# Layer 1's retention: queries decayed by VectorE out of the score banks, keys zero-padded to 128 rows, the head loop one half piece sooner

## The reference, cut to what matters

```python
def _retention_dir(q, k, v, log_g, inclusive):      # chunks of 128 tokens
    ...
    dmat = jnp.where(mask[None], jnp.exp(log_g[:, None, None] * jnp.maximum(diff, 0).astype(jnp.float32)), 0.0)
    xi = jnp.exp(log_g[:, None] * (n + 1).astype(jnp.float32))
    zeta = jnp.exp(log_g[:, None] * (RET_CHUNK - 1 - n).astype(jnp.float32))
    ...
    def step(state, qkv):
        qc, kc, vc = qkv
        inner = jnp.einsum('bhqk,bhkv->bhqv', jnp.einsum('bhqd,bhkd->bhqk', qc, kc) * dmat, vc)
        cross = jnp.einsum('bhqd,bhdv->bhqv', qc * xi[..., None], state)
        new_state = chunk_decay[:, None, None] * state + jnp.einsum('bhkd,bhkv->bhdv', kc * zeta[..., None], vc)
        return new_state, inner + cross
```

## Time and profile before

| what | us |
|---|---|
| three executions | 814.00, 814.11, 814.99 |
| median | 814.11 |
| span of the profiled execution, first to last instruction | 811.6 |
| TensorE busy in it | 805.4 (99%) |
| VectorE busy | 634.0 (78%) |
| ScalarE busy | 339.9 (42%) |
| GpSimd busy | 187.8 (23%) |

### The profile page before, as it was taken

How to read it: one execution, slowest core, us unless ns; L and a number is a source line. 1 busy time by engine, 2 the same in 40 slices (tenths; PEclk the granted TensorE clock), 3 DMA queues, 4 the chain that set the end, 5 groups by cost and what they waited for, 6 DMA issues and landing times.

```text
span 811.6 us, 11794 instructions
## 1 busy us (share of the span) xinstructions
PE 805.4 (99%) x4364; PEld 691.4 (85%) x4364; DVE 634.0 (78%) x1112; ACT 339.9 (42%) x721; POOL 187.8 (23%) x189
## 2 busy tenths in 40 slices
PE   9999999999999999999999999999999999999998
PEld 7788888888888888888888888888889988999986
DVE  5998778768984476885578788978798678599998
ACT  4374465632122254342545544551134222455580
POOL 2222111111121221122324555544260114000000
PEclk9999999999999999999999999999999999999999
DMA  7236644445143322336868677596935634866562
GB/s 241 88 96 233 233 155 156 151 161 182 53 156 114 95 78 78 90 93 130 177 144 163 140 151 161 131 182 135 202 104 183 182 98 135 235 184 183 184 203 78
DMA packets 132862, 120.47 MB, mean 148 GB/s; under 512 B 4749, under 2 KB 100550, under 8 KB 132806
## 3 DMA queue, kind: packets, MB, share of 16 engines
q1 hardware_dynamic: 124326, 102.94, 40.9%
q0 software_dynamic: 8448, 16.78, 12.4%
q10 hardware_dynamic: 32, 0.01, 0.0%
HBM read 117.62 MB, written 35.65 MB: 189 GB/s over the span
## 4 chain that ended last, share of the span: by engine, by line
PE 92%; DVE 5%; issue 1%; ACT 1%; DMA 1%; POOL 0%; DVEq 0%; ACTq 0%
PE proj L1886 23%; PE proj L1888 23%; PE proj L1887 23%; PE bank_t L1900 3%; PE bank_o L1975 2%; DVE x L1592 1%; PE score L1888 1%; PE score L1887 1%; PE score L1886 1%; DVE w_lo L1247 1%; PE score L2050 1%; PE score L1960 1%; PE score L1961 1%; PE score L2049 1%; PE bank_o L2068 1%
## 5 line engine op out<-in xcount | busy, mean ns | idle before, releaser
L1247 DVE TENSOR_TENSOR w_lo<-w_raw,w_hi 128x1024 fp32r<-128x1024 f32 x151 | 192.0, 1274 | 44.3 <-POOL w_hi L778 36.1
L778 POOL TENSOR_SCALAR w_hi<-w_raw 128x1024 fp32r<-128x1024 f32 x101 | 118.6, 1174 | 438.6 <-DMA w_raw<-in_w_in_dram 314.6
L1886 PE MATMUL proj<-xt_hi,w_hi 128*128 128x512 f32 (+1 forms) x448 | 171.2, 382 | 0.0
L1888 PE MATMUL proj<-xt_hi,w_lo 128*128 128x512 f32 (+1 forms) x448 | 168.1, 375 | 0.0
L1887 PE MATMUL proj<-xt_lo,w_hi 128*128 128x512 f32 (+1 forms) x448 | 167.8, 374 | 0.0
L1888 PEld LDWEIGHTS proj<-xt_hi,w_lo 128*128 128x128 f32 x448 | 84.4, 188 | 15.6
L1887 PEld LDWEIGHTS proj<-xt_lo,w_hi 128*128 128x128 f32 x448 | 84.5, 189 | 14.1
L1886 PEld LDWEIGHTS proj<-xt_hi,w_hi 128*128 128x128 f32 x448 | 84.5, 189 | 14.0
L1886 PE MATMUL proj<-w_hi,xt_hi 128*128 128x512 f32 x152 | 60.9, 401 | 0.2 <-ACT prob L1012 0.2
L1888 PE MATMUL proj<-w_hi,xt_lo 128*128 128x512 f32 x152 | 59.5, 391 | 0.0
L1887 PE MATMUL proj<-w_lo,xt_hi 128*128 128x512 f32 x152 | 59.4, 391 | 0.0
(11 more groups left out here) (471 smaller groups left out, 1871.2 us busy)
## 6 DMA issues: line engine op xcount, KB each, us to landing
w_raw<-in_w_in_dram SPq DMA_DIRECT2D x79, 512.0 KB, 3.8
w_sums<-in_w_in_dram SPq DMA_DIRECT2D x8, 1024.0 KB, 7.0
w_sums<-w_sums POOLq DMA_DIRECT2D x8, 1024.0 KB, 9.1
w_raw<-w_sums SPq DMA_DIRECT2D x16, 512.0 KB, 3.8
w_raw<-w_sums SPq DMA_DIRECT2D x32, 256.0 KB, 3.3
w_raw<-in_w_out_dram SPq DMA_DIRECT2D x14, 512.0 KB, 3.3
w_raw<-in_w_in_dram SPq DMA_DIRECT2D x26, 256.0 KB, 3.3
w_sums<-in_w_attn_out_dram SPq DMA_DIRECT2D x4, 1024.0 KB, 6.5
```

What stands on the lines that cost most here:

```text
L778: pool.tensor_scalar(hi, raw, 1.0, 1.0, ALU.mult, ALU.mult).then_inc(hi_done, 1)
L1247: dve.tensor_tensor(lo, raw, hi.bitcast(F32), ALU.subtract).then_inc(w_split, 1)
L1886: pe.matmul(out, left[0], right[0], start=first, stop=False)
L1888: return pe.matmul(out, left[1], right[0], start=False, stop=last)
```

## The change

Queries are turned undecayed (RT 2, 3 are what RT 6, 7 were), ACT copies them to rqT, and VectorE multiplies the same bank by `decays` (a new table, the decay of each of 128 tokens, same on all partitions) into q_decT: two directions by two heads, so four instructions of 64 x 512 for each RT, eight in all. RN 2, 3 and RT 4 to 7 are gone. The keys of each head get a tile of 128 rows, rk_own, with the other head's 64 rows set to zero: ACT copies each key bank twice, with a per-partition scale of ones and zeros (half_of), and RS contracts over 128 rows. `decays` is built by VectorE (one instruction of 128 x 128 for each direction and head beside dmat, and two to begin with) and exponentiated by ACT in one instruction of 128 x 1024. RT 0 to 3 now stand at g = 17 and 18 ahead of AV and AN; KV, RS, RA and RB of each head stand one to three halves sooner. In the new list g = 19 and 20 have no TensorE step, g = 21 is KV 0, RS 0, F 0 in this order, and g = 22 is F 1.

```diff
 DA_FIRST = 4 * U_RQK
-RET_FIRST = DA_STEPS + 6
-RET_NORMS = (RET_FIRST + 3, RET_FIRST + 5, RET_FIRST + 9, RET_FIRST + 11)
+RET_FIRST = DA_STEPS + 5
+RET_NORMS = (RET_FIRST + 3, RET_FIRST + 5, RET_FIRST + 7, RET_FIRST + 9)
 WIN_FIRST = 4 * U_Z0 + 5
...
     g = 2 * (n - DA_FIRST) + half
+    x = 2 * (g - DA_STEPS - 1)
+    if 0 <= x < 4:
+        out += [("RT", x), ("RT", x + 1)]
     if 3 <= g < DA_STEPS + 3:
...
         out.append(("RN", g - 10))
-    if g == DA_STEPS:
-        out += [("RN", 2), ("RN", 3)]
-    x = 2 * (g - DA_STEPS - 1)
-    if 0 <= x < 8:
-        out += [("RT", x), ("RT", x + 1)]
     h, odd = divmod(g - RET_FIRST, 2)
...
             out.append(("RA", h - 1))
-    finals = {21: 0, 22: 1, 23: 2, 25: 3, 27: 4, 29: 5, 34: 6, 36: 7}
+    finals = {21: 0, 22: 1, 23: 2, 25: 3, 27: 4, 29: 5, 32: 6, 34: 7}
     if g in finals:
...
         diff = sb("diff", [P, TAB], stack=one)
-        rkT = sb("rkT", [P, 2, S], stack=one)
         k_decay = sb("k_decay", [P, ST, RET_HEADS, 2, HD], stack=one)
         dmat = sb("dmat", [P, RET_HEADS, P], stack=one)
+        decays = sb("decays", [P, 2, RET_HEADS, P], stack=one)
         lam_s = sb("lam_s", [P, 2], stack=one); lam_e = sb("lam_e", [P, 2], stack=one); neg_lam = sb("neg_lam", [P, 1], stack=one)
...
         dec_z = sb("dec_z", [P, 8], stack=one); dec_q = sb("dec_q", [P, 8], stack=one); dec_p = sb("dec_p", [P, 8], stack=one)
-        log_g = sb("log_g", [P, 8], stack=one); steps_to = sb("steps_to", [P, 4], stack=one)
-        ret_c = sb("ret_c", [P, 6, RET_HEADS], stack=one); rs_k = sb("rs_k", [P, ST], stack=one)
+        log_g = sb("log_g", [P, 8], stack=one); steps_to = sb("steps_to", [P, 2], stack=one); half_of = sb("half_of", [P, 2], stack=one)
+        ret_c = sb("ret_c", [P, 4, RET_HEADS], stack=one); rs_k = sb("rs_k", [P, ST], stack=one)
         neg_log_b = sb("neg_log_b", [P, 4], stack=one)
...
         decay_arg = sem("decay_arg"); decay_done = sem("decay_done")
-        ret_scaled = sem("ret_scaled")
+        ret_scaled = sem("ret_scaled"); q_decayed = sem("q_decayed"); halves_set = sem("halves_set")
         rt_done = sem("rt_done"); rt_free = sem("rt_free")
...
                 act.wait_ge(rt_done, m + 1)
-                if m == 6:
+                if m == 0:
+                    act.wait_ge(halves_set, 4)
+                if m == 2:
                     act.wait_ge(av_done, DA_STEPS)
-                dst = rkT[:, m, :] if m < 2 else q_decT[:, m - 2, :] if m < 6 else rqT[:, m - 6, :]
-                act.activation(dst, score[:, m % 2, :], ACT.Copy).then_inc(rt_free, 1)
+                if m < 2:
+
+                    for c in range(2):
+                        last = act.activation(rk_own[:, 2 * m + c, :], score[:, m % 2, :], ACT.Copy, scale=half_of[:, c:c + 1])
+                else:
+                    last = act.activation(rqT[:, m - 2, :], score[:, m % 2, :], ACT.Copy)
+                last.then_inc(rt_free, 1)
...
                         act.activation(dmat[:], dmat[:], ACT.Exp).then_inc(decay_done, 1)
+                        act.activation(decays[:], decays[:], ACT.Exp).then_inc(decay_done, 1)
...
                 minus_p = diff[:, CENTRE:CENTRE + 1]
-                for k, (sign, steps) in enumerate(((-1.0, 1.0), (1.0, P), (1.0, P - 1.0), (-1.0, 0.0))):
+                for c in range(2):
+                    here, there = halves(c)
+                    dve.memset(half_of[here, c:c + 1], 1.0).then_inc(halves_set, 1)
+                    dve.memset(half_of[there, c:c + 1], 0.0).then_inc(halves_set, 1)
+                for k, (sign, steps) in enumerate(((1.0, P - 1.0), (-1.0, 0.0))):
                     dve.tensor_scalar(steps_to[:, k:k + 1], minus_p, sign, float(steps), ALU.mult, ALU.add).then_inc(dve_chain, 1)
                     chain[0] += 1
                 dve.wait_ge(dve_chain, chain[0])
-                for k in range(4):
-                    dve.tensor_scalar(ret_c[:, k, :], log_g[:, 4 * (k % 2):4 * (k % 2) + 4], steps_to[:, k:k + 1], None, ALU.mult)
-                dve.tensor_scalar(ret_c[:, 4:6, :], log_g[:].rearrange("p (c h) -> p c h", c=2), float(P), None, ALU.mult).then_inc(decay_arg, 1)
+                for k in range(2):
+                    dve.tensor_scalar(ret_c[:, k, :], log_g[:, 4 * k:4 * k + 4], steps_to[:, k:k + 1], None, ALU.mult)
+                last_row = RET_HEADS - 1
+                done(dve.tensor_scalar(decays[:, 0, last_row, :], diff[:, CENTRE:CENTRE + P], minus_p, 1.0, ALU.subtract, ALU.add))
+                done(dve.tensor_scalar(decays[:, 1, last_row, :], decays[:, 0, last_row, :], -1.0, P + 1.0, ALU.mult, ALU.add))
+                dve.tensor_scalar(ret_c[:, 2:4, :], log_g[:].rearrange("p (c h) -> p c h", c=2), float(P), None, ALU.mult).then_inc(decay_arg, 1)
...
                 near = diff[:, CENTRE:CENTRE + P]
+                for c in range(2):
+                    dve.tensor_scalar(decays[:, c, h, :], decays[:, c, RET_HEADS - 1, :], log_g[:, 4 * c + h:4 * c + h + 1], None, ALU.mult)
                 done(dve.tensor_scalar(dmat[:, h, :], near, neg_log_b[:, h:h + 1], None, ALU.mult))
...
                                 wait_evacuated(dve, U_RQK, j)
-                        c = m % 2
-                        src = rqk[:, :, 256:512] if m < 2 else rqk[:, :, 0:256]
-                        dve.tensor_tensor((k_decay if m < 2 else q_decay)[:, :, :, c, :], src.rearrange("p s (h d) -> p s h d", h=RET_HEADS),
-                                          ret_c[:, 2 + c if m < 2 else c, :].unsqueeze(1).unsqueeze(3).broadcast_to([P, ST, RET_HEADS, HD]),
+                        dve.tensor_tensor(k_decay[:, :, :, m, :], rqk[:, :, 256:512].rearrange("p s (h d) -> p s h d", h=RET_HEADS),
+                                          ret_c[:, m, :].unsqueeze(1).unsqueeze(3).broadcast_to([P, ST, RET_HEADS, HD]),
                                           ALU.mult).then_inc(ret_scaled, 1)
+                    elif kind == "RT" and m >= 2:
+
+                        if m == 2:
+                            dve.wait_ge(decay_done, 3)
+                        dve.wait_ge(rt_free, m + 1)
+                        for c in range(2):
+                            here, h = slice(c * HD, (c + 1) * HD), 2 * (m - 2) + c
+                            for d in range(2):
+                                last = dve.tensor_tensor(q_decT[d * HD:(d + 1) * HD, h, :].rearrange("p (s q) -> p s q", s=ST),
+                                                         score[here, m % 2, :].rearrange("p (s q) -> p s q", s=ST),
+                                                         decays[here, d, h, :].unsqueeze(1).broadcast_to([HD, ST, P]), ALU.mult)
+                        last.then_inc(q_decayed, 1)
                     elif kind == "KV":
...
                         for k in (1, 2):
-                            dve.scalar_tensor_tensor(out=state[k + 1][f, :], in0=state[k][f, :], scalar=ret_c[f, 4, m:m + 1],
+                            dve.scalar_tensor_tensor(out=state[k + 1][f, :], in0=state[k][f, :], scalar=ret_c[f, 2, m:m + 1],
                                                      in1=kv[k][f, :], op0=ALU.mult, op1=ALU.add)
-                            back = dve.scalar_tensor_tensor(out=state[2 - k][b, :], in0=state[3 - k][b, :], scalar=ret_c[b, 5, m:m + 1],
+                            back = dve.scalar_tensor_tensor(out=state[2 - k][b, :], in0=state[3 - k][b, :], scalar=ret_c[b, 3, m:m + 1],
                                                             in1=kv[3 - k][b, :], op0=ALU.mult, op1=ALU.add)
...
                             wait_evacuated(pe, U_RQK, j)
-                    if m == 2:
-                        pe.wait_ge(ret_scaled, 4)
                     for s in range(ST):
                         if m < 2:
                             src = rqk[:, s, 256 + m * P:256 + (m + 1) * P]
-                        elif m < 6:
-                            src = q_decay[:, s, m - 2, :, :].rearrange("p c d -> p (c d)")
                         else:
-                            src = rqk[:, s, (m - 6) * P:(m - 5) * P]
+                            src = rqk[:, s, (m - 2) * P:(m - 1) * P]
                         last = pe.transpose(score[:, m % 2, s * P:(s + 1) * P], src, ident[:])
...
                     if m == 0:
-                        pe.wait_ge(rt_free, 8)
+                        pe.wait_ge(rt_free, 4)
+                        pe.wait_ge(q_decayed, 1)
+                        pe.wait_ge(ret_scaled, 2)
                         for j in range(ST):
...
                         pe.wait_ge(kr_free, 2 * m)
-                    r = slice((m % 2) * HD, (m % 2 + 1) * HD)
+                    else:
+                        pe.wait_ge(q_decayed, 2)
                     for c in range(ST):
-                        last = pe.matmul(score[:, 1, c * P:(c + 1) * P], rkT[r, m // 2, c * P:(c + 1) * P],
-                                         rqT[r, m // 2, c * P:(c + 1) * P], start=True, stop=True)
```

(4 more changed lines are left out.)

## The result

The changed kernel takes 830.69 us (median; 828.49 to 832.15), before 814.55 beside it: ratio 1.0189, interval 1.0164 to 1.0213, so 16.1 us slower. The profiled execution took 828.49 us, the shortest of the four; its span is 826.5, against 811.6 before.

A forecast was written before the change was run, and what follows sets the result against it. TensorE, busy 99% of the span, was taken to bound the kernel. Saving -3.5, waits +1.3 and +4.9, a pause +0.7, clock or third wait +1.5 gave +4.9: 814.1 to 819.0 us, range 816.2 to 822.4.

The forecast's parts named there:

- TensorE's saving: TensorE loses 3.5 us: 1.74 for RT 4 to 7, 1.4 for RS, 0.36 for fewer starts behind steps.
- the 1.4 for the padding: RS over 128 rows instead of 64 runs as AV does, saving 0.35 us per head, 1.4 for four.
- Rival 3: Padded keys give nothing, RS stays at 1.09 us, forecast otherwise holds: +0.8, 819.8 us; 12%.
- VectorE at g = 18: Eight multiplications ahead of AN, 0.61 us apiece, 4.9 in all, from 172.3 to 177.2.
- a pause: VectorE's small instructions sometimes take 0.7 us more; one taken in the gapless chain from 172.3 to 191.0.
- The waits at F 0 and F 1: TensorE waits 1.3 us at F 0 for ON 0 and 4.9 at F 1 for F 0 taken out.
- Rivals 1 and 2: 1: all VectorE work stays hidden, 810.6 us, 8%. 2: VectorE's multiplications cost half, 814.5 us, 8%.
- 5: Rival: the change doesn't do what it says, transposes stay or keys aren't padded; near 820 us, 1%.
- Rival 4: Both clock (2.4 us) and third wait (1.6 left at F 7), with two pauses: +8.1, 822.2 us; 10%.
- The third wait: TensorE at F 7 waits 0 to 2.6 us for F 6 taken out; 1.5 taken together with the clock.
- The clock: TensorE's clock may halve in the 4.9 us wait, costing 2.4 if lasting as long; 1.5 shared with third wait.

The follow-up runs named there:

- late multiplications: Changed kernel with retention at its old places, ACT copying queries to both halves, VectorE multiplying 128 x 512 per head at g = 21, 23, 25, 27: 814.68 us, ratio 0.9987.
- padded keys alone: Kernel before with only each head's keys on 128 rows, other head's 64 zero, and scores over 128 rows; places as before: 814.86 us, ratio 0.9992.

## Why the prediction was right and wrong

Slower was right; 16.1 instead of 4.9 lies outside my range.

**TensorE's saving.** 2.5 us in the changed kernel and 2.6 with late multiplications, against 3.5. RS at 0.89 and KV to RS at 0.88 came as forecast. The stretch shows 0.9 of the 1.4 for the padding. Rival 3 is out. The rule of the Trainium skill that I set against it ("TensorE: Matmul & The Clock Gate", Part 2: for the time of a weight load the number of rows doesn't matter) is about the load alone, and there the trace agrees: a load of RS took 188 ns over 64 rows and 192 over 128. What I drew from it for rival 3, that padding gives nothing, was wrong. The gain is in when a load begins: the first of RS over 64 rows began with its matmul (both at 185.69), the first over 128 rows 0.10 ahead of it (186.40 and 186.50, padded keys alone).

**VectorE at g = 18.** Start 172.90 (forecast 172.3), each 0.70 and not 0.61: I took from RN that an instruction begins 0.08 before the last ends, and these don't. End 178.5, not 177.2. With two pauses instead of one F 0 was taken out 1.96 later than forecast (192.96 against 191.0). I had priced a pause as one that comes for no reason that the rows show; it comes where a GpSimd instruction runs, and GpSimd's timeline would have told which rows to look beside.

**The waits at F 0 and F 1.** 2.9 and 5.5, 8.4 together, where I had 1.3, 4.9 and 0.7 for a pause, 6.9: right places and right causes, 1.5 too little for want of those sizes. Rivals 1 and 2 are out, and 5 with them (sixteen matmuls are gone). Rival 4 came nearest, with two pauses and both the clock and a third wait, but it had that wait at F 7 and only 1.6 long.

**The third wait: the step that failed.** I weighed VectorE's work from F 0 to F 6 against TensorE's, and looked for a wait at F 7 alone, of 0 to 2.6 and sharing a term with the clock. F 6 and F 7 waited for nothing. The wait came at the first piece of w_out, for a gate tile, 5.0. I had asked what a moved step now stands ahead of on its queue for KV 0 and RS 0, but not for RB 2 and RB 3, which moved three halves, past VectorE's taking of the last gate tiles. RB 3 back in its place took 3.4 off the wait and 6.6 off the median time.

**The clock.** I took 1.5 for it and a third wait together, and 2.4 if the half clock lasts as long as the wait. It fell twice, for 1.55 and 1.4, and the half clock did not last as long as the wait. The Trainium skill's rule (same page, Part 1: the throttled state is the default, activity releases it) agrees with the trace in the middle of the kernel too, in the waits of 5.5 and 5.0. It would have been worth a term of its own for each long wait.

Steps against the forecast, in the stretch: saving -2.5 (-3.5), F 0 2.9 (1.3), F 1 5.5 (4.9, and the 0.7 of a pause), gate tile 5.0 and clock 2.95 (1.5 together): +13.9 (+4.9). The third wait and the two falls are 6.5 of the 9 missed. The other 2.2 between this and the 16.1 are 1.0 of the span outside the stretch and the 1.2 by which the medians differ more than the spans.

## What to carry to other kernels

Where an order is written out by hand, list for every step that is moved all that its engine does between its old and its new place, evacuations of projection banks too, and look up who waits for each. Before work goes on an engine ahead of a serial chain, ask whether it is needed there: with the multiplications ahead of the attention's norm the kernel lost 4.1 us, and with them in larger instructions spread behind it nothing that can be measured. Before work goes from VectorE to GpSimd, look in the trace at what VectorE's rows do beside a GpSimd instruction. A TensorE wait of 4 us or more is priced with the clock's return, 1.3 to 2.3 us here; one of 2 to 3 us may or may not be.

## What the runs showed of the hardware that was not expected

- TensorE's granted clock fell to 0.50 in or just behind every wait of 3.9 us and more (3.9, 4.4, 4.6, 4.9, 5.0, 5.3, 5.5 twice, 9.0). Of the shorter ones it fell with 2.0 and one of 2.9, and stayed at 1.00 with 2.1, 2.7 twice and the other of 2.9. A fall cost 1.3 to 2.3 us of slow matmuls after the restart.
- VectorE's pauses end with GpSimd's instructions: a 128 x 4 of 0.17 us took 0.89 beside a GpSimd instruction of 1.07 and ended with it, as did all 24 such pauses of before's trace.
- VectorE's 64 x 512 out of a score bank with a broadcast operand begin 0.70 apart, 128 x 512 out of SBUF 0.60: half the partitions saved nothing.
- GpSimd's 128 x 512 multiplication took 1.73 on average (1.31 to 2.23), VectorE's 0.67, and VectorE's own instructions beside them took 4.0 longer in all.
- RS over 64 rows took 1.09 for eight, over 128 rows 0.89, though a weight load took 188 and 192 ns.
